# A hybrid DeltaNet and sliding-window layer: small transposes regrouped on TensorE, and new orders at the unit ends

## What is computed

```python
h = jnp.einsum('btd,dc->btc', x, w_in)                      # all input projections
ya = _deltanet_group(qa, ka, va, za, ba, aa, conv_w, ...)   # 4 heads of 128, chunked, gated by silu(za)
yb = _swa_group(qb, kb, vb, zb, sinks)                      # 8 query heads of 64, window 128, gated by silu(zb)
y = jnp.einsum('btc,cd->btd', jnp.concatenate([ya, yb], -1), w_out)
return _layernorm(DEEPNORM_ALPHA * x + y, ln_g, ln_b)
```

## Time and profile before

| | |
|---|---|
| median of 3 runs | 1087.4 us |
| lowest and highest run | 1086.05 and 1089.49 us |
| time of the profiled run | 1086.05 us |
| its span, first to last instruction | 1084.2 us |
| PE busy | 1056.9 us (97%) |
| DVE busy | 708.2 us (65%) |
| ACT busy | 497.1 us (46%) |
| POOL busy | 115.6 us (11%) |
| granted TensorE clock, mean | 0.997 |

### The profile page before, as it was taken

How to read it: one execution, slowest core, us unless ns; L and a number is a source line. 1 busy time by engine, 2 the same in 40 slices (tenths; PEclk the granted TensorE clock), 3 DMA queues, 4 the chain that set the end, 5 groups by cost and what they waited for, 6 DMA issues and landing times.

```text
span 1084.2 us, 19346 instructions
## 1 busy us (share of the span) xinstructions
PE 1056.9 (97%) x7116; PEld 837.3 (77%) x7116; DVE 708.2 (65%) x2180; ACT 497.1 (46%) x1509; POOL 115.6 (11%) x152
## 2 busy tenths in 40 slices
PE   7999999999999999999999999999999999999997
PEld 5878777868778787776887878777787878787885
DVE  5286858685566757667366665767637576768665
ACT  4566566654636343352252535435344545353300
POOL 3423132133200000010000000002000000002310
PEclk9999999999999999999999999999999999999999
DMA  8867484764653726253453471715445343622332
GB/s 276 306 228 263 157 282 176 263 202 168 218 184 128 240 80 230 93 185 99 168 197 133 125 246 51 259 63 186 132 160 178 127 157 127 210 76 87 118 117 78
DMA packets 58430, 183.55 MB, mean 169 GB/s; under 512 B 8480, under 2 KB 21216, under 8 KB 45024
## 3 DMA queue, kind: packets, MB, share of 16 engines
q1 hardware_dynamic: 58192, 182.05, 48.9%
q10 hardware_dynamic: 144, 0.26, 0.1%
HBM read 138.22 MB, written 44.07 MB: 168 GB/s over the span
## 4 chain that ended last, share of the span: by engine, by line
PE 49%; DVE 4%; DMA 3%; issue 1%; POOL 0%; SPq 0%; ACT 0%; DVEq 0%
PE bank L857 24%; PE bank L908 8%; PE bank L1153 4%; PE bank L965 1%; PE bank L1003 1%; PE bank L1136 1%; DMA y_tile<-y_spill 1%; PE bank L1121 1%; DMA x_stage<-xT 1%; DVE y_cols L1840 1%; DVE y_step L1836 1%; PE bank L1131 1%; PE bank L1137 1%; PE bank L1129 1%; PE bank L980 1%; PE bank L1058 1%
## 5 line engine op out<-in xcount | busy, mean ns | idle before, releaser
L857 PE MATMUL bank<-xr,w 128*128 128x512 f32 x2496 | 656.1, 406 | 7.7 <-DVE xr L1552 7.7
L857 PEld LDWEIGHTS bank<-xr,w 128*128 128x128 f32 x2496 | 451.4, 189 | 103.0 <-issue 9.9
L908 PE MATMUL bank<-wo,y_split 128*128 128x512 f32 x432 | 114.5, 404 | 0.0
L908 PEld LDWEIGHTS bank<-wo,y_split 128*128 128x128 f32 x432 | 77.0, 189 | 14.7 <-issue 0.7
L1605 DVE SCALAR_TENSOR_TENSOR kq<-conv_in,convw_all,kq 128x512 f32<-128x512 f32 x96 | 75.2, 783 | 6.8 <-ACT conv_in L1207 5.7
L1369 ACT ACTIVATE score<-score,neg_max 128x128 f32<-128x128 f32 (+1 forms) x128 | 52.6, 414 | 31.8 <-DVE neg_max L1794 31.8
L1505 ACT ACTIVATE o_scaled<-bank 128x128 f32<-128x128 f32 x64 | 17.7, 276 | 99.6 <-PE bank L1137 99.4
L1980 DVE SCALAR_TENSOR_TENSOR state<-state,cols_all,bank 128x128 f32<-128x128 f32 x64 | 22.2, 348 | 61.8 <-PE bank L1136 61.8
L1836 DVE TENSOR_TENSOR y_step<-blocks,y_cols 128x60 f32<-128x60 f32 (+14 forms) x240 | 50.4, 210 | 12.3 <-DMA blocks<-n_spill 3.5
L791 POOL TENSOR_TENSOR xr<-y_tile,xr 128x256 fp32r<-128x256 f32 x8 | 7.6, 981 | 451.4 <-ACT xr L1188 451.4
L1974 DVE TENSOR_SCALAR steps<-bank,nb_rk 128x128 f32<-128x128 f32 x64 | 22.3, 348 | 47.5 <-PE bank L1131 47.5
(11 more groups left out here) (225 smaller groups left out, 1653.6 us busy)
## 6 DMA issues: line engine op xcount, KB each, us to landing
w<-w_split SPq DMA_DIRECT2D x78, 1024.0 KB, 5.5
w_split<-w SPq DMA_DIRECT2D x26, 1024.0 KB, 5.2
blocks<-n_spill SPq DMA_DIRECT2D x32, 256.0 KB
y_spill<-y_out SPq DMA_DIRECT2D x30, 256.0 KB, 5.5
x_tile<-w_in SPq DMA_DIRECT2D x13, 512.0 KB, 6.1
y_tile<-w_in SPq DMA_DIRECT2D x12, 512.0 KB, 6.1
y_tile<-y_spill SPq DMA_DIRECT2D x12, 512.0 KB, 6.3
x_tile<-x SPq DMA_DIRECT2D x12, 512.0 KB, 3.9
```

What stands on the lines that cost most here:

```text
L857: ins = nc.tensor.matmul(bank[JOBS[at].bank][:], w[:, turn % 3, wp, k, :], xr[:, xp, k], start=(step == 0), stop=(step == 3 * KT - 1))
L908: ins = nc.tensor.matmul(bank[JOBS[at].bank][:], y_place(t)[:, yp, k], wo[:, k, wp, half * UNIT:(half + 1) * UNIT], start=(step == 0), sto ...
```

## The change

Slots 0 to 3 keep their order. Call a slot *joined* when `n >= 4` and `i < 3` (nine slots: 4, 5, 6, 8, 9, 10, 12, 13, 14).

- In joined slots the v and output transposes (1067, 1072) move behind the first `turns` (980), without dense steps between.
- From slot 4 on, the first product of the last level (1101) is issued at `at.turns1`, right ahead of the second `turns`. In slots 7 and 11 it moves behind 7 dense steps from beside line 884.
- On DVE, `gate_a` moves in joined slots from ahead of `divide` to behind `part_band`; in unit ends from slot 7 on, `part_band` moves ahead of the `add_half` that stands there.
- On ACT, the copies of the job "k" come ahead of `v_tok` in joined slots.
- On SP, `load_x(s+1, 3)` moves ahead of `load_blocks` in slots 7 and 11; in slot 12 the weight load moves from ahead of `load_blocks` to behind `spill_a`.

```diff
--- before.py
+++ after.py
@@ SP, slot @@
-                if i == 0 and n > 0:
+                if i == 0 and 0 < s < SBS - 1:
                     after_jobs(n, JOBS[JOB_AT["q", n + 1]].end - n)
+                if i == AH - 1 and 0 < s < SBS - 1:
+                    x_split(sp, s + 1, 0)
+                    load_x(s + 1, 3)
                 load_blocks(n)
...
-                if i == AH - 1 and 0 < s < SBS - 1:
-                    x_split(sp, s + 1, 0)
-                    load_x(s + 1, 3)
@@ PE, slot @@
-                fill_to(n, AT_VTOK)
+                joined = n >= AH and i < AH - 1
+                if joined:
+                    fill_to(n, at.turns0)
+                    turns(n, 0)
+                else:
+                    fill_to(n, AT_VTOK)
                 after(pe, prep_ready, n, 2)
...
-                fill_to(n, at.turns0)
-                turns(n, 0)
+                if not joined:
+                    fill_to(n, at.turns0)
+                    turns(n, 0)
...
-                fill_to(n, at.p64)
+                fill_to(n, at.p64 if n < AH else at.turns1)
@@ ACT, slot @@
+                if n >= AH and i < AH - 1:
+                    after_jobs(n, 0.25)
                 after(act, vtok_done, n, 1)
@@ DVE, slot @@
-                if n > 0 and n != AH - 1:
+                joined = n >= AH and i < AH - 1
+                if n > 0 and n != AH - 1 and not joined:
                     gate_a(n - 1)
...
+                if n >= AH and i == AH - 1:
+                    part_band(n, 0)
                 after_jobs(n, at.base)
-                if n >= AH:
+                if joined:
                     part_band(n, 0)
+                    gate_a(n - 1)
```

## The result

The changed kernel took **1088.35 us** in the median of 20 runs (1084.15 to 1099.69). The kernel before, run beside it, took 1083.99 us (20 runs, 1081.38 to 1089.49). The ratio is **1.0056**, with a 95% interval of 1.0034 to 1.0078: it is slower by 0.6%, where 1082.3 us and a gain had been forecast. The ratio follows the means (1090.4 beside 1084.4 us, 6.0 us apart) more than the medians (4.4 us apart), because several runs of the changed kernel took 1091 to 1100 us. Its runs spread over 15.5 us, those of before over 8.1.

The account below looks back on a forecast made before the run. PE, busy 97% of the span, was taken as the bound. Gains of 7.9 us less costs of 1.5 and 1.3 made 5.1 off 1086.05, so 1080.95, plus 1.35 to the median: 1082.3 us, range 1079.5 to 1086.7.

Parts of the forecast that it names:

- `gate_a` late on SP: Slots 5, 6, 9, 10: late spill delays the y load, tile slips 0.5 us; cost 1.2 us, bounds 0 and 8.3.
- The rival of the full slip: Line 1090, slots 4, 5, 6, 8, 9, 10: y tile slips in full, 1092.4 us, slower; chance 0.10.
- The starting point: Whole kernel: profiled run of 1086.05 us, with the median of the runs taken as 1.35 us above it.
- Slot 7: Earlier x load ends line 872's wait for POOL and its clock loss; gain 4.1 us, bounds 2 and 4.5.
- The contention with POOL: Slots 7 and 11: held harmless; as rival, `part_band` slows POOL's first piece, 0.9 us lost each, 1084.1 us; chance 0.08.
- Slots 11, 12 and 15: Waits of line 1080 shrink through earlier base inverses, earlier blocks and `part_band` filling a DVE wait: gains 0.7, 1.7, 0.5 us.
- late blocks: Unit ends: blocks land late behind the x load, slot 7 gains 2 us, slot 11 nothing; 1085.1 us, chance 0.15.
- late weights: Slots 12 to 14: weight load behind `spill_a` late by 1 us each; 1085.3 us, chance 0.08.
- Joined runs: Nine slots: one run of 27 dense steps takes 6.21 us instead of 6.38; gain 0.08 us a slot, 0.7 in all.
- The first turns: Turns 0.79 us earlier wait for scaled weights: 0.35 us in slots 12 to 14, 0.5 in slot 4; cost 1.5 us.

Follow-up runs that it names:

- the unit ends alone: Kernel before plus only the moved x load, slot 12's new load order and `part_band` ahead in slots 7, 11 and 15: 1080.33 us, ratio 0.9960.

## Why the prediction was wrong, point by point

**The step that failed: "`gate_a` late on SP".** The place was right, even the mechanism (the spill waits for the gate, the tile slips), and the term was sized at 1.2 us where the four slots of the profiled run lost 12.1. Three things in it were wrong.

- *The slip.* I took 0.5 us, "what the queue runs dry between the weights and the late spill", as the engines were full. Measured: 1.9 us in the mean. The step "the tile's landing is the end of a backlog whose sum does not change" failed. The dry stretch itself was about what I took (0.6 us in slot 6), but the weights ahead of the tile landed 2.1 us later in the mean and the tile with them. The earlier trace rows show the transfers in their old order, with weights and store issued early; the change holds these back as well, and moves the spill from 4 us ahead of the weights to right ahead of them. An average over the old order says nothing on a stretch where the transfers start later. How the 1.9 us divide stays open.
- *Who waits.* I looked at line 1090 only. In slots 6 and 10 the output product's first step (908) stands ahead of line 1096 and waits for the tile's low part itself: 2.0 and 0.3 us.
- *The clock.* I had charged it to slot 7, where I took it off (1.2 + 0.4 us; the missing clock there comes to 1.7), and did not charge it to the waits I added: 6.8 us in the profiled run. My upper bound of 8.3 us for this term was near the waits (6.4), but without the clock it was no bound: the term came to 12.1.

The rival of the full slip named the right line and the right size of the slip (1.9 us, where it eats all of the gain), and priced the kernel at 1092.4 us. The median is 1088.35. Slots 4 and 8, which it charged with 1.5 us each, did not pay (in slot 8 the tile landed at 573.05, 0.7 us later into the slot than before, and nothing waited), and its 8.3 us lack the clock; that it is within 4 us is in part luck. It was given 0.10, because the slip was argued from the mean share of the engines.

**The starting point** was high as well. The sum starts from the median of three runs, 1087.4 us; over 20 runs the kernel before has 1083.99, 2.1 us *below* its profiled run and not 1.35 above. So the forecast of 1082.3 meant a gain of 5.1 us, and against a loss of 4.4 us the miss is 9.5 us by the medians, more than the 6 us between 1088.35 and 1082.3.

**What held.** *Slot 7*: 4.1 us forecast, 3.9 measured between the two profiled runs. The mechanism is right, the size in part luck: it is the worth of the edit beside a run that had the long wait of line 872, and three of five profiles with the old order did not have it. There the edit is worth 0.7 to 1.1 us. Line 872 waits no more, POOL's second piece follows the first, and the 19 dense steps run at full clock, to be read beside the earlier trace rows:

```profile
491.73 3.88 PE L872 MATMUL bank<-xr,ba_w 128*16 128x512 f32 x16
495.45 4.51 PE L857 MATMUL bank<-xr,w 128*128 128x512 f32 x19
...
501.53 0.45 PE L1086 MATMUL bank<-steps,n_t 32*32 32x32 f32 x32 [0.55 <-DVE steps L1856]
```

```profile
487.51 3.80 POOL L791 TENSOR_TENSOR xr<-y_tile,xr 128x256 fp32r<-128x256 f32 x4 [199.63 <-ACT xr L1194]
491.27 2.84 POOL L791 TENSOR_TENSOR xr<-x_stage,xr 128x256 fp32r<-128x256 f32 x4
```

```profile
495.45:499.89 4.44, 4.44 (x20) 3.38 (x18) 3.69 (x20) 0.97 (x3) 0.00 (x0) 1.00 0.00 0
```

*The contention with POOL* did not come, as forecast: `part_band` beside POOL's first piece took what it takes alone in slot 5 (0.68 us), and the piece kept its 3.80 us. The Trainium skill (GPSIMD Engine Reference, Specifications) names DVE instructions in a two-port mode or with two SBUF inputs as contending with GpSimd. With `part_band`'s one input from PSUM the trace agrees.

```profile
488.54 0.68 DVE L1825 TENSOR_TENSOR score<-bank,past 128x512 f32<-128x512 f32 x1
```

*Slots 11, 12 and 15*: 0.7, 1.7 and 0.5 us forecast; 0.6, 1.4 (with the first turns' 0.35 in it) and 0.6 measured. The gains of the unit ends stand in the run of these alone as well, -7.0 us in these four slots of its profile, but the medians give back only 4.1 us of it. That is a second, smaller miss of the forecast: the profiled run of before (1086.05 us), with its long wait in slot 7, was 2.1 us above its median, and the one of the unit ends alone 1.7 us below its own.

*The rivals of late blocks and of late weights* did not come: line 1086 waited 0.55 and 0.52 us in slots 7 and 11, and PE waited for no weights in the short slots.

*Joined runs*: a run of 27 dense steps takes 6.25 us to the next group in slot 5, and v and output transposes 0.44 and 0.35, where 6.21 was forecast.

```profile
347.37 6.42 PE L857 MATMUL bank<-xr,w 128*128 128x512 f32 x27
353.62 0.60 PE L980 MATMUL bank<-ident,score 128*128 128x128 f32 x4
```

*The first turns* pay in the short slots 13 and 14 what was forecast (0.35 us each): 0.4 and 0.3 us; in slot 4 it is 0.9 (0.5 forecast). In slot 13 the wait does not show as an idle time but inside the group, 0.83 us long instead of 0.60:

```profile
882.23 0.83 PE L980 MATMUL bank<-ident,score 128*128 128x128 f32 x4
```

## What to carry to other kernels

When a wait on a DMA queue grows, list everything that stands behind it up to the next transfer with a deadline, megabytes first: here the tile with the deadline was 1.9 us late behind weights that were 2.1 us late, and a DMA share near 1 in the old trace was no cover, since it was made by the very issues that are now late. An order on a queue that no data needs (here tile behind spill) is the cheapest thing to change: it turned a loss of 0.6% into a gain of 0.3%. When you move a transfer, look for who waits for the buffer that it reads, or the test measures that wait instead. Put the clock into the upper bound of a new wait of TensorE: here it took 1.7 or 3.4 us in three of the four slots with new waits, as much as the waits themselves. And look at more than one profile of the kernel before: a wait of 2.9 us that only some runs have is worth less than it shows.

## What was not expected of the hardware

**The clock falls in lumps.** In every profiled run that lost any clock in slots 5 to 12, a slot lost 1.7 or 3.4 us: slots 6 (3.4), 9 and 10 (1.7 each) of the changed kernel, slot 7 of the one before (1.7), or slot 5 of the kernel with the gate ahead of `part_band` (1.7, after a wait of 1.53 us). But whether a given wait brings a fall is not settled: a wait of 1.9 us in slot 9 of that last kernel brought none, nor one of 1.69 us in slot 12 before; one of 1.75 us at the same place in the kernel with the last level's product alone did (1.7), and 1.00 us in slot 10 of the changed kernel did too, after 0.30 us shortly before. This is a likely reason for much of the changed kernel's spread of 15 us, which shrank to 2 us with the waits gone: the ten faster of its 20 runs have a mean granted clock of 0.9975, the ten slower one of 0.993, which makes 5 us of the 7.4 us between their mean times. It was not tested by itself.

**The landing comes after the engines have gone quiet.** In slot 6 of the changed kernel the DMA engines were busy for 0.07 from 428.80 to 431.00, and yet the tile was there only at 431.82. Before the tile, the same queue had written an output tile and the spill to DRAM. The Trainium skill (DMA: Bandwidth & Descriptors, Queues, rings and completion order) says that a transfer's signal lands only after every earlier write of that DMA engine; that would fit. The signal of the spill came long before, 20.9 us into the slot, that of the output tile's store at 28.6 us, in the same quiet stretch; and with the spill behind the tile the stretch from 26 to 28 us of slot 6 was as quiet (share 0.14), with the tile there at 29.6 us. So if an earlier write held the tile back, it was not the spill's; no run here took the store away alone, and the cause stays open. With the same order of issues on SP, the landing moves by up to 2 us from slot to slot (26.6 to 28.7 us in the kernel with the last level's product alone), so a landing that has less than that to spare should be counted as late in some runs.
